# Where the conditioning of layer 1 is multiplied: multiply-adds on VectorE, or small matmuls on TensorE, beside the MLP of layer 0

## The reference

```python
def trunk_layer(x, cvec, ctx_kv, lp):
    mods = jnp.split(jax.nn.silu(cvec) @ lp['w_ada'] + lp['b_ada'], 6, axis=-1)   # (2048,) @ (2048, 12288)
    sh1, sc1, g1, sh2, sc2, g2 = [m[:, None, :] for m in mods]
    h = rms_norm(x, lp['g_pre1']) * (1.0 + sc1) + sh1
    z = h @ lp['w_in']
    ...                                             # attention, pooling, convolution -> mix, through w_out
    x = x + g1 * rms_norm(mix, lp['g_post1'])
    h = rms_norm(x, lp['g_pre2']) * (1.0 + sc2) + sh2
    f = jnp.square(jax.nn.relu(h @ lp['w_mlp1'])) @ lp['w_mlp2']                  # 2048 -> 8192 -> 2048
    x = x + g2 * rms_norm(f, lp['g_post2'])
```

## Time and profile before

| what | value |
| --- | --- |
| median of three runs | 3635.08 us |
| span of the profiled execution, first to last instruction | 3632.8 us |
| PE busy / DVE busy / ACT busy / POOL busy | 3313.9 / 2253.9 / 1182.0 / 894.1 us |
| mean granted TensorE clock | 0.949 of full speed |
| DVE products of the conditioning of layer 1 (L1126, 1440 of them) | 658.2 us busy |
| `w_low` (L750, 672 of them) | 911.4 us busy |

### The profile page before, as it was taken

The page is one execution under the profiler, slowest core; times in us unless marked ns, Lnnn a source line. Parts: engine busy times, 40 slices in busy tenths (PEclk is TensorE's granted clock), DMA queues, the critical chain, the costliest instruction groups (busy, mean ns, idle before and its releaser), DMA issues.

```text
span 3632.8 us, 54989 instructions
## 1 busy us (share of the span) xinstructions
PE 3313.9 (91%) x19515; PEld 3099.7 (85%) x19515; DVE 2253.9 (62%) x3459; ACT 1182.0 (33%) x1539; POOL 894.1 (25%) x523
## 2 busy tenths in 40 slices
PE   6899999779999999999995988894999999999997
PEld 3588767669999999999994977683999999999996
DVE  1357654498889889888898596537333334333334
ACT  2122343322333333323332324442333333333333
POOL 1047000432122122222234291024111111111114
PEclk8799999889999999999997999997999999999998
DMA  8855566436666666666651432130443444444342
GB/s 282 285 186 185 188 222 217 141 110 193 217 201 195 200 210 207 193 197 216 201 188 41 136 108 76 53 96 27 130 130 121 127 127 127 127 125 126 125 126 69
DMA packets 562192, 566.15 MB, mean 156 GB/s; under 512 B 17784, under 2 KB 559088, under 8 KB 561680
## 3 DMA queue, kind: packets, MB, share of 16 engines
q1 hardware_dynamic: 559776, 560.02, 48.7%
q0 software_dynamic: 1344, 4.33, 0.4%
q10 hardware_dynamic: 944, 0.32, 0.0%
HBM read 560.93 MB, written 3.67 MB: 155 GB/s over the span
## 4 chain that ended last, share of the span: by engine, by line
PE 61%; DVE 16%; issue 12%; DMA 4%; POOL 3%; ACT 3%; SPq 1%; DVEq 0%; ACTq 0%; POOLq 0%
PE ps L1170 54%; DVE ada_sums L1126 5%; DMA ada_raw<-in_w_ada_dram 3%; DVE w_lo L750 2%; POOL z L406 2%; PE ps L1180 2%; DVE full L822 2%; DVE x L803 1%; PE ps L1230 1%; DVE conv L918 1%; ACT w_hi L513 1%; POOL z L502 1%; PE ps L1210 1%; DMA raw<-in_w_in_dram 1%; ACT prob L633 1%
## 5 line engine op out<-in xcount | busy, mean ns | idle before, releaser
L750 DVE TENSOR_TENSOR w_lo<-raw,w_hi 128x1024 fp32r<-128x1024 f32 x672 | 911.4, 1361 | 951.0 <-ACT w_hi L513 940.9
L1170 PE MATMUL ps<-h_hi,w_hi 128*128 128x384 f32 x3328 | 1135.6, 341 | 74.3 <-DVE h_lo L811 68.9
L1170 PE MATMUL ps<-h_lo,w_hi 128*128 128x384 f32 x3328 | 1120.8, 337 | 0.0
L1170 PE MATMUL ps<-h_hi,w_lo 128*128 128x384 f32 x3328 | 1120.5, 337 | 0.0
L513 ACT ACTIVATE w_hi<-raw 128x1024 fp32r<-128x1024 f32 x672 | 709.7, 1057 | 1050.3 <-PE ps L1170 1011.3
L1170 PEld LDWEIGHTS ps<-h_hi,w_hi 128*128 128x128 f32 x3328 | 631.4, 190 | 107.9 <-issue 97.9
L1170 PE MATMUL ps<-hid_hi,w_hi 128*128 128x384 f32 x2048 | 694.0, 339 | 0.0
L1170 PE MATMUL ps<-hid_lo,w_hi 128*128 128x384 f32 x2048 | 691.1, 337 | 0.0
L1170 PE MATMUL ps<-hid_hi,w_lo 128*128 128x384 f32 x2048 | 690.6, 337 | 0.0
L1126 DVE SCALAR_TENSOR_TENSOR ada_sums<-ada_raw,cond,ada_sums 128x256 f32<-128x256 f32 x1440 | 658.2, 529 | 0.0
L1170 PEld LDWEIGHTS ps<-h_lo,w_hi 128*128 128x128 f32 x3328 | 631.6, 190 | 0.3
(11 more groups left out here) (174 smaller groups left out, 2201.9 us busy)
## 6 DMA issues: line engine op xcount, KB each, us to landing
raw<-in_w_mlp_dram SPq DMA_DIRECT2D x512, 512.0 KB, 3.7
ada_raw<-in_w_ada_dram SPq DMA_DIRECT2D x384, 512.0 KB, 4.6
raw<-in_w_in_dram SPq DMA_DIRECT2D x96, 512.0 KB, 4.5
raw<-in_w_out_dram SPq DMA_DIRECT2D x64, 512.0 KB, 3.5
out_dram<-y_rows SPq DMA_DIRECT2D x12, 256.0 KB, 2.4
staged<-in_x_sample_dram SPq DMA_DIRECT2D x1, 2048.0 KB, 10.2
pw_w<-in_w_conv_pw_dram POOLq DMA_DIRECT2D x2, 1024.0 KB, 6.3
staged<-in_x_prompt_dram SPq DMA_DIRECT2D x1, 1024.0 KB, 5.0
```

The source lines that it names most:

```text
L750: nc.vector.tensor_tensor(w_lo[:, j % 4, :, :], raw[:, j % 4, :, :], w_hi[:, j % 4, :, :].bitcast(F32), ALU.subtract).then_inc(lo_ready, 1)
L1170: last = nc.tensor.matmul(ps[:, 2 * pair + t, 0:TOK], w[:, j % 4, k, P * t:P * t + P], v[:, kt + k, :], start=begin and k == 0 and i == 0, ...
```

## The change

The blocks of layer 1 are multiplied as those of layer 0 are. `ada_products` and `turn_sums` are gone, and `ada_sums` with them. In a quad of the first MLP that has a block, PE runs `ada_unit` for pieces 0 and 1 after unit 0, for pieces 2 and 3 after unit 1, and `ada_turn` after unit 3. DVE copies the bank ahead of `w_low` of unit 2 and adds the bias after that of unit 3. The loads, their order and the waits in SP's text stay; `ada_used`, on which they wait, is now counted up by PE in the quad of the block itself, and no longer by DVE in the quad before.

```diff
-        ada_sums = new("ada_sums", [2, 2, UC])
+        top[0] += 4 * (TOK + UC + 2 * P)
...
-                def ada_products(ch, block, j, mark0):
-                    n, k0 = ch * 6 + (ADA_BLOCKS + block), mark0 + 28 * block + 7 * j
-                    dve.wait_ge(ada_landed[j], 16 * (n + 1))
-                    if j == 0:
-                        dve.wait_ge(ada_turned, n - 1)
-                    for o in range(8):
...
-                        if j or k:
-                            op = nc.vector.scalar_tensor_tensor(out=out, in0=ada_raw[:, j, k, :], scalar=cond[:, 4 * j + k, g:g + 1],
-                                                                in1=out, op0=ALU.mult, op1=ALU.add)
...
+                    ada = first and k in ADA_OF_QUAD
+                    if ada:
+                        m = ch * 6 + ADA_OF_QUAD[k]
                     for j in range(4):
                         if k == 3 and j == 3:
                             hidden_low(2 * k, ch * 4 + (k + 32 * layer))
+                        if ada and j == 2:
+                            ada_copy(m + ADA_BLOCKS)
                         if j < prefetch:
                             w_low(j, ch * Q_CHUNK + quad(layer, Q_MLP + k + 1))
                         if k < 3 and j == 3:
                             hidden_low(2 * k, ch * 4 + (k + 32 * layer))
-                        if first and k + 1 in ADA_OF_QUAD:
-                            ada_products(ch, ADA_OF_QUAD[k + 1], j, mark0)
-                        if first and k in ADA_OF_QUAD and j == 3:
-                            m = ch * 6 + ADA_OF_QUAD[k]
+                        if ada and j == 3:
                             ada_mods(1, m, m + ADA_BLOCKS)
...
-            def turn_sums(n, buffer):
-                pe.wait_ge(ada_used, 4 * n + 4)
-                pe.wait_ge(mods_ready, n)
-                for t in range(2):
-                    for g in range(2):
-                        last = nc.tensor.matmul(ps[:, BANK_MOD, 2 * t + g:2 * t + g + 1], ada_sums[:, buffer, g, P * t:P * t + P],
-                                                ones[:, 0:1], start=True, stop=True)
-                last.then_inc(ada_turned, 1)
...
                                 unit(j, q, j // 2, 4 * (j % 2), hid_hi, hid_lo, j % 2 == 0, j % 2 == 1)
-                            if first and k in ADA_OF_QUAD and j == 2:
-                                turn_sums(ch * 6 + (ADA_OF_QUAD[k] + ADA_BLOCKS), ADA_OF_QUAD[k] % 2)
+                            if first and k in ADA_OF_QUAD:
+                                n = ch * 6 + (ADA_OF_QUAD[k] + ADA_BLOCKS)
+                                for u in {0: (0, 1), 1: (2, 3)}.get(j, ()):
+                                    ada_unit(n, u)
+                                if j == 3:
+                                    ada_turn(n)
```

More of the change, by code:

```diff
@@ L1110, in hidden_low, with mlp_quad @@
                                             ALU.subtract).then_inc(hid_ready, 1)
-                def ada_products(ch, block, j, mark0):
-                    n, k0 = ch * 6 + (ADA_BLOCKS + block), mark0 + 28 * block + 7 * j
-                    dve.wait_ge(ada_landed[j], 16 * (n + 1))
-                    if j == 0:
-                        dve.wait_ge(ada_turned, n - 1)
-                    for o in range(8):
[L1119 to L1124, removed]
-                        if j or k:
-                            op = nc.vector.scalar_tensor_tensor(out=out, in0=ada_raw[:, j, k, :], scalar=cond[:, 4 * j + k, g:g + 1],
-                                                                in1=out, op0=ALU.mult, op1=ALU.add)
[L1128 to L1132, removed]
+                def mlp_quad(ch, k, prefetch=4):
+                    ada = first and k in ADA_OF_QUAD
+                    if ada:
+                        m = ch * 6 + ADA_OF_QUAD[k]
                     for j in range(4):
@@ L1140, in mlp_quad @@
                             hidden_low(2 * k, ch * 4 + (k + 32 * layer))
-                        if first and k + 1 in ADA_OF_QUAD:
-                            ada_products(ch, ADA_OF_QUAD[k + 1], j, mark0)
-                        if first and k in ADA_OF_QUAD and j == 3:
-                            m = ch * 6 + ADA_OF_QUAD[k]
+                        if ada and j == 3:
                             ada_mods(1, m, m + ADA_BLOCKS)
                 last_layer = layer == DEPTH - 1
-                n0 = chain.n
                 with dve.Fori(0, CHUNKS - 1 if last_layer else CHUNKS) as ch:
                     for k in range(Q_CHUNK):
-                        mlp_quad(ch, k, ch * 168 + n0)
-                if first:
-                    chain.n = n0 + CHUNKS * 168
+                        mlp_quad(ch, k)
                 if last_layer:
                     for k in range(Q_CHUNK):
-                        mlp_quad(CHUNKS - 1, k, 0, prefetch=0 if k == Q_CHUNK - 1 else 4)
+                        mlp_quad(CHUNKS - 1, k, prefetch=0 if k == Q_CHUNK - 1 else 4)
                 inverse_root(4 * layer + 3)
```

## The result

The changed kernel takes 3690.02 us (median; 3681.30 to 3690.85, 4 runs) against 3633.33 of the kernel before on the same chip: ratio **1.0152** (95% interval 1.0134 to 1.0170), slower. The forecast was 3664, with a range to 3680: so the time lies outside the range. The sign was right, and half of the loss was missed. The profiled execution has a span of 3689.0 us, 56.2 more than before.

The account below looks back on a forecast made before the run. PE was taken as the bound, with DVE close to it in the first MLP: 1066.66 + 135.7 = 1202.4 us in place of 1172.65, +29.7, less 0.95 after the MLP, so 3635.1 + 28.8 = 3664 us; range 3654 to 3680.

Parts of the forecast that it names:

- What the conditioning cost before: First MLP on PE: 43.2 us of `turn_sums` and 62.8 us from waits for DVE, 105.99 us, all taken as removed.
- What is added on PE: First MLP: 96 groups of two pieces at 1.143 us and 47 turns at 0.553 us add 135.7 us.
- What a group costs: PE's groups of pieces: one piece 0.78 us, the second 0.36 more; some 0.4 us per group pays for changing tiling mode.
- DVE's copies and the loads, at nothing: First MLP: 48 DVE copies, 20 us, stay off PE's path; reordered loads keep over 10 us of cover.
- After the MLP, -0.95 us: Wait for GpSimd between last unit and first sum of squares falls from 5.53 us to layer 1's 4.58.
- The floor is that of layer 1, so a chunk takes 150.3 us: First MLP: layer 1's 1066.66 us plus 135.7 gives 1202.4 us, chunks of 150.3 us on average.
- C: Rival: weights reach PE late behind pieces' loads in 32 quads following one with a block; 3696 to 3843 us; 8 in 100.
- D: Rival: the 23 us no row names are waits for ScalarE or GpSimd and return; up to 3687 us; 7 in 100.
- B: Rival: mode changes beside the MLP cost nothing, so pieces are cheaper; 3614 us; 6 in 100, with other ways to be faster.
- E: Rival, no difference: pieces and turns in the first MLP cost 112 us in place of 135.7; 3640 us; 5 in 100.

Follow-up runs that it names:

- e4: Kernel before, DVE's products of layer 1's conditioning on 128 of 256 columns, first half's sums taken twice: 3568.9 us, ratio 0.9824.
- e8: Changed kernel, quads 5 to 7 of PE's chunk loop written once and looped over in both layers: 3660.9 us, ratio 1.0081 to the kernel before.
- e9: As e8, with the four pieces of a block in one group behind unit 0: 3644.9 us, ratio 1.0030 to the kernel before.
- e1: Changed kernel, quads 5 to 7 of PE's chunk loop written once and looped over in layer 0 only: 3686.2 us, ratio 1.0149 to the kernel before.
- e2: Kernel before, PE's loop of layer 1's MLP written out for two chunks, four passes in place of eight: 3640.8 us, ratio 1.0022.

## Where the prediction was right, and the step that failed

*What the conditioning cost before* (105.99 us, all of it removable): right. e4 leaves 1.3 us besides the turns, and PE has no wait for DVE in the changed kernel.

*What is added on PE* (135.7 us, a group 1.14, a turn 0.55): right in mechanism and size. In e8 the MLP of layer 0 is 1204.92 - 1066.55 = 138.4 us longer than that of layer 1, 2.7 more than forecast; by the quads in the chain it is 2.86 in place of 2.84 each. A chunk of e8 takes 150.48 us from the second on, for a forecast of 150.3, and the first 151.77.

*What a group costs*, 0.4 us for the change of form and 0.36 for each further piece: right in kind, the change forecast too dear (14.3 us for 48 groups in e9, 0.30 each).

*DVE's copies and the loads, at nothing*: right. ScalarE does wait for weights in the first MLP (84.3 us over 21 times), and PE never for `w_lo`.

*After the MLP, -0.95 us*: wrong, though small. Between the last unit and the sums lie 1990.89 - 1985.36 = 5.53 us, as before.

*The floor is that of layer 1, so a chunk takes 150.3 us*: **this is the step that failed.** It counted what PE executes and took for granted that its text is there. The new text is 84 matmul instructions a chunk longer (96 and 12 for 24), and the seven back edges then cost 33.9 us, 4.8 each on average, of which 2.7 are the wait (18.9 / 7) and nearly all of the rest the lower clock behind it (13.7 / 7 = 2.0). The prediction had no term for this; a chunk takes 154.9 us on average. With it removed (e8) the time is 3660.9, for a forecast of 3664. That this is so near is in part luck: by the profiles e8's first MLP is 32.3 us longer than before, where 29.7 were forecast, but its median is only 26.7 us above that of the kernel before beside it (3634.3).

The rivals: C (loads) and D (waits that stay) are refuted by e1, which leaves both as they were. B asked for a group under 0.84 us; by the chain of the changed kernel groups cost 1101.19 - 1095.89 - 4.167 = 1.13 us and 1106.56 - 1101.19 - 4.167 = 1.20, so E, which had them at 1.00, is out as well.

The Trainium skill has the rule that the prediction did not weigh ("Runtime: NRT & Kernel Launch", Instruction fetch mechanics): each engine has a memory for a limited piece of its text, TensorE 128 KiB or 2048 instructions, filled in blocks of 16 KiB (256 instructions), and a taken branch whose target is not in a window of two blocks has to wait for a fetch. The runs agree in the block, 1.08 MB / 66 = 16 KB a packet, and in the wait. They do not agree with a window of two blocks: the loop of layer 1 has 768 matmuls in a pass, more than the 512 instructions of two blocks, and runs through seven back edges with 3 packets in the kernel before; here the measurement decides. Where a loop is fetched, a pass brings 154 KB in the changed kernel and 147 KB in e1, both more than 128 KiB (131 KB). That the text of layer 1 takes up nine blocks in one place and eight in another would explain the shifts; this is an estimate from 63 / 7 = 9 packets and from that page's 128 KiB, and not shown.

## What to carry to other kernels

A change that adds instructions to a loop that fills its engine changes two things, what is executed and how long the text is; read the instruction queues in the page before and after, and where PE's waits are as many as the loop's back edges, whether they name "issue" or a copy, suspect fetches and test it with a shorter text. Write the like parts of a long loop body once, in an inner loop: here that was worth 29 us and cost nothing that the profile shows. And where work is moved between two engines of which each would become the bound, divide it: two blocks of six on TensorE, with a text that is held, gave 0.9% over none of them, and all six, with the same care (e9), lost 0.3%.

## What the runs showed that was not expected

- Text that nobody changed can become slower by its place alone: the MLP of layer 1 takes 1091.3 us in e1 and 1067.9 with 16 idle matmuls in front of it.
- Fetching costs at the back edge only: 2.7 us each in e2, 3.5 in layer 1 of e1 and 4.8 in the changed kernel. Within a pass of 1536 matmuls it costs nothing (e2), although 52 packets come for three back edges there.
- A wait of 2.60 us is followed by 120 matmuls that take 23.87 us, where 20.94 is usual: there the lower clock adds as much again as the wait. It doesn't follow every wait: behind one of 2.94 us only 0.15 is lost, and in layer 1 of e1, where PE waits 1.1 to 1.9 us twice at each back edge, the clock stays full.
